# Branches for an expert's further blocks taken once per unit of weights, and their activations transposed in the next pass

## The chip, the core and the metric

The kernel runs on one core of a Trainium2 chip. Its time is the device time of one launch, in microseconds (us); a lower one is better. The engines are TensorE (PE; its weight loads are shown apart, as PEld, and its sequencer as PEldq), VectorE (DVE), ScalarE (ACT), GpSimd (POOL) and SyncE (SP), which here only issues DMAs. Each engine has an instruction stream of its own; they meet at semaphores.

## The reference

One decoder layer on 512 tokens of 1024 channels, in float32. After a token-mixing sub-layer (two attentions, some 500 us here, not touched) comes a mixture of 32 experts of which each token uses four:

```python
top_val, top_idx = lax.top_k(logits, TOP_K)            # 4 of 32, softmax weights
padded = (counts + MOE_BLOCK - 1) // MOE_BLOCK * MOE_BLOCK   # groups by expert, blocks of 128 rows
def expert_block(args):
    xb, e = args                                       # 128 tokens of expert e
    gu = xb @ w_gate_up[e] + b_gate_up[e]              # 1024 -> 2048
    return clamped_swiglu(gu) @ w_down[e] + b_down[e]  # 1024 -> 1024
```

How many tokens an expert gets is known only at run time: 2048 token slots over 32 experts, 64 on the mean, one to four blocks of 128 each.

## The kernel before

**Tiling.** An expert's weights come as 12 halves of 1 MB (512 rows by 512 columns each): eight for gate and up, four for down. Two halves make a unit, one output of 128 tokens by 512 columns. For float32 accuracy each half is split into a high and a low part: ACT copies it to `wh` (L1154, a ring of four), DVE subtracts (L1225, in place of the raw half, a ring of eight), and `multiply` (L1048) issues 12 matrix multiplications for a half and a block: high by high, low by high, high by low, over four chunks of 128 rows. A bias matmul (L1057) opens each unit.

**Passes.** `passes` (L940) runs the experts: number 0 by itself, then a loop of 15 passes with two experts each, then number 31 and a tail. In the pass of expert e, PE runs gate and up of e, transposes the tokens of e+1 (`tokens_transposed`, L996), runs down of e-1 and transposes the activations of e (`act_transposed`, L1027). The token blocks are gathered and scattered by POOL.

**Further blocks.** Nearly all experts have one block (b = 0). Code for b = 1, 2, 3 stands in the program all the same, inside nested run-time branches (`further`, L908: `with self.eng.If(self.more >= 1)`). `x.blocks(work)` puts the further blocks ahead of block 0, `x.first_then_further(work)` behind it. PE calls it for each half (`gate_up_half_used` eight times, `down_half_used` four times) and for both transposes, so PE has 14 such branches an expert, all on line L909; for an expert with one block each of them jumps over its code. The wait for the half's low part (`wl_done`) stands ahead of the branch. The loop's own branch is on L943; a hint at the loop's top names it.

**Order.** Everything is in the order of the code; nothing is scheduled. `half_used` frees a half's place for the next load (SP, L973) and for ACT's next copy.

Of the kernel before, what the change touches and what calls it, by code (L numbers as in the profile page):

```python
# [23 lines left out]
P = 128  # L24
# [8 lines left out]
E = 32  # L33
# [58 lines left out]
def program(nc, ctx, x, c, rel_bias_table, w_ada, b_ada, g_mix_pre, g_mix_post, g_ffn_pre, g_ffn_post, w_in, w_out,  # L92
# [895 lines left out]
    def experts_pe(pe):  # L988
        pe.wait_ge(nk_ready, 1)

        def transposed(b, src, done):
            for k in range(KC):
                ins = nc.tensor.transpose(turned(b)[:, k // 4, (k % 4) * P:(k % 4 + 1) * P], src[:, k * P:(k + 1) * P], ident[:])  # L993
            ins.then_inc(done[min(b, 1)], 1)

        def tokens_transposed(x, e):  # L996
# [5 lines left out]
            def work(b):  # L1002
                if b == 0:
                    pe.wait_ge(xg_in[0], (e + 1) * 16)
                else:
                    if b == 1 and not begins:
                        acts = Expert(pe, e - 1).prefix() + START
                        if not (isinstance(e, int) and e == 1):
                            outputs = Expert(pe, e - 2).prefix() * U_D + START
                        pe.wait_ge(al_done[1], acts)  # L1010
# [10 lines left out]
                transposed(b, xy[b], xt_done)  # L1021
# [37 lines left out]
        def gate_up_half_used(x, has_d, place, v):  # L1059
            t, up, h = v // 4, v // 2 % 2, v % 2  # L1060
            pe.wait_ge(wl_done, place.count(v))

            def work(b):
                dst = summed(b, up)
                if v == 0 and b == 0:
                    pe.wait_ge(xl_done[0], x.count(1, 0, 0))
                if v == 0 and b:
# [6 lines left out]
                if h == 0:  # L1074
                    if b == 0:
                        if t == 0 and has_d:
                            pe.wait_ge(y_half_copied[up], x.e - 1 + START)
                        elif t:
                            pe.wait_ge((u_ready if up else g_ready)[0], x.count(T_GU, 0, 0))
# [10 lines left out]
                elif h:  # L1090
                    ins.then_inc(gu_more, 1)
# [755 lines left out]
```

## Time and profile before

| | us |
|---|---|
| median of 3 runs | 1965.25 |
| lowest, highest | 1964.48, 1971.41 |
| profiled execution: device time | 1966.11 |
| its span in the trace | 1964.3 |
| PE busy in the span | 1700.9 |
| expert loop, from PE's first to its last matmul in it | about 514 to 1900 |

The profile comes from one execution. A row of PE's timeline gives a matmul's start and its modelled length; since matmuls overlap, the distance from one start to the next is what it costs. "issue" as the releaser of an idle time means that the trace shows nothing that the engine waited for. Branches and register instructions are the sequencer's, and are not counted as busy, but their own lengths can be read on their lines.

### The profile page before, as it was taken

The page shows a single profiled execution, that of the slowest core. Times are in us where ns is not written, and L with a number is a line of the kernel's source. Part 1 is how long each engine was busy: PE and PEld are TensorE (multiplying, and loading weights), DVE is VectorE, ACT ScalarE, POOL GpSimd, SP SyncE. Part 2 cuts the span into 40 slices and gives each one's busy share as a digit, 9 for nine tenths or more (in the row PEclk, how much of TensorE's full clock was granted, in tenths as well). Part 3 has the DMA queues.
Part 4 walks back from the last instruction along what each step waited for, and adds up shares of the span by engine and source line. Part 5 has one row for each costly group of instructions (what it writes and reads, how often), then busy time and mean ns, then how long its engine had stood idle before and what let it go on. Part 6 is the DMA issues. An engine that isn't in the chain of part 4 may idle for free.

```text
span 1964.3 us, 24736 instructions
## 1 busy us (share of the span) xinstructions
PE 1700.9 (87%) x7526; PEld 1315.3 (67%) x7527; DVE 1317.5 (67%) x1024; ACT 1029.6 (52%) x922; POOL 229.2 (12%) x232
## 2 busy tenths in 40 slices
PE   6999976685488999999999999999999998989860
PEld 1788854443376877787777877878787787778650
DVE  0444468644478778586877877866687787566645
ACT  2322234511366766465766766745576676455530
POOL 2000000102201001011111101101100111001110
PEclk9999987797699999999999999999999999999885
DMA  7675440012689999687989988977798899667735
GB/s 230 218 246 185 150 120 1 28 65 76 230 300 333 326 327 337 221 300 279 353 309 323 353 315 319 370 255 259 273 373 317 315 362 331 219 237 274 274 135 220
DMA packets 245582, 498.81 MB, mean 254 GB/s; under 512 B 16795, under 2 KB 17927, under 8 KB 244737
## 3 DMA queue, kind: packets, MB, share of 16 engines
q1 hardware_dynamic: 228288, 458.26, 65.5%
q0 software_dynamic: 14448, 34.73, 5.2%
q8 instruction: 217, 3.56, 0.7%
q10 hardware_dynamic: 2610, 2.11, 0.3%
q14 instruction: 19, 0.16, 0.0%
HBM read 490.23 MB, written 27.09 MB: 263 GB/s over the span
## 4 chain that ended last, share of the span: by engine, by line
PE 69%; issue 5%; DVE 3%; DMA 2%; ACT 1%; POOL 1%; POOLq 0%; ACTq 0%; DVEq 0%
PE ps L1051 20%; PE ps L1052 20%; PE ps L1053 19%; PE ps L621 3%; PE ps L993 3%; PE ps L1057 3%; DMA x1e<-x_after_mixing 1%; ACT wh L1154 1%; DVE wl L1225 1%; DMA xy<-h_ffn,icur 1%; DMA expert_rows<-xy,icur 1%; PE ps L641 0%; DVE yo L1388 0%; PE ps L634 0%; ACT h2t L692 0%
## 5 line engine op out<-in xcount | busy, mean ns | idle before, releaser
L1225 DVE TENSOR_TENSOR wl<-rawm,wh 128x2048 fp32r<-128x2048 f32 x384 | 876.2, 2290 | 318.9 <-ACT wh L1154 316.9
L1154 ACT ACTIVATE wh<-rawm 128x2048 fp32r<-128x2048 f32 x384 | 736.2, 1918 | 488.9 <-PE ps L1053 488.8
L1051 PE MATMUL ps<-wh,xh 128*128 128x512 f32 x1120 | 477.8, 427 | 0.0
L1052 PE MATMUL ps<-wl,xh 128*128 128x512 f32 x1120 | 447.4, 399 | 0.0
L1053 PE MATMUL ps<-wh,xl 128*128 128x512 f32 x1120 | 446.3, 399 | 0.0
L1053 PEld LDWEIGHTS ps<-wh,xl 128*128 128x128 f32 x1120 | 216.9, 194 | 48.2
L1052 PEld LDWEIGHTS ps<-wl,xh 128*128 128x128 f32 x1120 | 217.9, 195 | 45.6
L1051 PEld LDWEIGHTS ps<-wh,xh 128*128 128x128 f32 x1120 | 219.3, 196 | 41.6
L1051 PE MATMUL ps<-wh,ah 128*128 128x512 f32 x560 | 235.0, 420 | 0.0
L1052 PE MATMUL ps<-wl,ah 128*128 128x512 f32 x560 | 220.4, 394 | 0.0
L1053 PE MATMUL ps<-wh,al 128*128 128x512 f32 x560 | 220.1, 393 | 0.0
L1331 POOL COPY icur<-stab 128x1 int32 (+1 forms) x35 | 49.6, 1417 | 1026.4 <-ACT xy L1194 1026.3
L1057 PE MATMUL ps<-bparts,sel 96*128 96x512 bf16 x210 | 85.1, 405 | 70.3 <-issue 54.8
L1053 PEld LDWEIGHTS ps<-wh,al 128*128 128x128 f32 x560 | 106.4, 190 | 23.3
L1052 PEld LDWEIGHTS ps<-wl,ah 128*128 128x128 f32 x560 | 106.8, 191 | 21.9
L1051 PEld LDWEIGHTS ps<-wh,ah 128*128 128x128 f32 x560 | 107.5, 192 | 20.3
L1711 DVE TENSOR_TENSOR wlf<-raw,whf 128x2048 fp32r<-128x2048 f32 (+1 forms) x18 | 39.1, 2174 | 100.7 <-ACT whf L1487 100.7
L1057 PEld LDWEIGHTS ps<-bparts,sel 96*128 (+1 forms) x210 | 20.5, 98 | 115.3 <-issue 110.3
L1590 PE MATMUL ps<-whf,hh 128*128 128x512 f32 (+1 forms) x192 | 71.3, 372 | 0.0
L1592 PE MATMUL ps<-whf,hl 128*128 128x512 f32 (+1 forms) x192 | 71.1, 370 | 0.0
L1591 PE MATMUL ps<-wlf,hh 128*128 128x512 f32 (+1 forms) x192 | 71.0, 370 | 0.0
L993 PE MATMUL ps<-ident,xy 128*128 128x128 f32 x280 | 38.4, 282 | 33.2 <-DMA xy<-h_ffn,icur 26.8
(224 smaller groups left out, 1658.2 us busy)
## 6 DMA issues: line engine op xcount, KB each, us to landing
rawm<-in_w_gate_up SPq DMA_DIRECT2D x256, 1024.0 KB, 6.6
rawm<-in_w_down SPq DMA_DIRECT2D x128, 1024.0 KB, 6.3
raw<-in_w_ada SPq DMA_DIRECT2D x24, 1024.0 KB, 5.3
raw<-in_w_in SPq DMA_DIRECT2D x16, 1024.0 KB, 5.2
yt<-expert_rows POOLq DMA_DIRECT2D x4, 2048.0 KB, 9.1
wo<-in_w_out SPq DMA_DIRECT2D x2, 2048.0 KB, 17.0
bias_vectors_repeated<-bias_vectors POOLq DMA_DIRECT2D x1, 2304.0 KB, 15.8
xs<-in_x ACTq DMA_DIRECT2D x1, 2048.0 KB, 24.5
```

Of the source, the lines that this page charges most:

```text
L621: ins = nc.tensor.matmul(ps[:, 2 * b + half, :], src[:, k, t * P:(t + 1) * P], wo[:, 4 * b + k, half * UN:(half + 1) * UN], start=(k == 0) ...
L993: ins = nc.tensor.transpose(turned(b)[:, k // 4, (k % 4) * P:(k % 4 + 1) * P], src[:, k * P:(k + 1) * P], ident[:])
L1051: nc.tensor.matmul(dst, a_h[:, b, kk, :], wh[:, place.split(v), k, :], start=False, stop=False)
L1052: nc.tensor.matmul(dst, a_h[:, b, kk, :], wl[:, place.slot(v), k, :], start=False, stop=False)
L1053: ins = nc.tensor.matmul(dst, a_l[:, b, kk, :], wh[:, place.split(v), k, :], start=False, stop=kk == KC - 1)
L1057: nc.tensor.matmul(dst, sel[:, bass.ds(e, 1)].to_broadcast([96, P]), bias, start=True, stop=False)
L1154: nc.scalar.activation(flat(wh[:, place.split(v), :, :]), flat(rawm[:, place.slot(v), :, :]), ACT.Copy).then_inc(wh_done, 1)
L1225: nc.vector.tensor_tensor(flat(wl[:, place.slot(v), :, :]), flat(rawm[:, place.slot(v), :, :]), flat(wh[:, place.split(v), :, :]), ALU.sub ...
L1331: nc.gpsimd.tensor_copy(icur[:, 1, b:b + 1], stab[:, b, bass.ds(x.e + 1, 1)]).then_inc(scur[m], 1)
L1590: nc.tensor.matmul(dst, a_h, b_h, start=first, stop=False)
L1591: nc.tensor.matmul(dst, a_h, b_l, start=False, stop=False)
L1592: return nc.tensor.matmul(dst, a_l, b_h, start=False, stop=last)
```

## The change

On PE the work of an expert is asked for once per unit and not once per half: `gate_up_used` (four calls) and `down_used` (two) have one branch each for the further blocks, with both halves of the unit inside it, then block 0 with both halves. The wait for a half's low part now stands ahead of that half's own matmuls. The first block's activations are transposed inside the second down unit, between its halves (`first_act_transposed`). Those of the further blocks are transposed in the next pass, ahead of its second unit (`further_act_transposed`, a branch of its own), and a branch ahead of the fourth unit waits that they are split (`further_acts_split`). ACT and DVE split them behind the second half of the next pass. The further blocks' activations all use the same two PSUM banks. PE now has nine branches an expert instead of 14. No matmul, transpose, copy or DMA is added or removed. `multiply` and `biased` are as they were.

```diff
--- before.py
+++ after.py
-        def transposed(b, src, done):
+        def transposed(banks, src, done):
             for k in range(KC):
-                ins = nc.tensor.transpose(turned(b)[:, k // 4, (k % 4) * P:(k % 4 + 1) * P], src[:, k * P:(k + 1) * P], ident[:])
-            ins.then_inc(done[min(b, 1)], 1)
+                ins = nc.tensor.transpose(banks[:, k // 4, (k % 4) * P:(k % 4 + 1) * P], src[:, k * P:(k + 1) * P], ident[:])
+            ins.then_inc(done, 1)
...
-        def act_transposed(x, last):
+        def first_act_transposed(x, last):
 
             pe.wait_ge(xl_done[0], x.e + (1 if last else 2) + START)
-
+            pe.wait_ge(act_ready[0], x.count(T_GU, 1, 0))
+            transposed(turned(0), actv[:, 0, :], at_done[0])
+
+        def further_act_transposed(x):
             def work(b):
-                if b == 1:
-                    tokens = x.before + x.more if last else Expert(pe, x.e + 2).prefix()
-                pe.wait_ge(act_ready[min(b, 1)], x.count(T_GU, 1, b))
-                if b == 1:
-                    pe.wait_ge(xl_done[1], tokens + START)
-                    pe.wait_ge(y_copied[1], x.before * U_D + START)
-                if b == 2:
-                    pe.wait_ge(al_done[0], x.count(1, 0, 0))
-                if b == 3:
-                    pe.wait_ge(al_done[1], x.count(1, 0, b) - 2)
-                transposed(b, actv[:, b, :], at_done)
-                if b == 2:
-                    pe.wait_ge(al_done[1], x.count(1, 0, b))
-                    pe.sem_inc(passed, 1)
-            x.first_then_further(work)
+                pe.wait_ge(act_ready[1], x.count(T_GU, 1, b))
+                pe.wait_ge(al_done[0], x.count(1, 0, 0))
+                pe.wait_ge(al_done[1], x.count(1, 0, b) - 1)
+                transposed(turned(0), actv[:, b, :], at_done[1])
+            x.further(work)
+
+        def further_acts_split(x):
+            with pe.If(x.more >= 1):
+                x.prefix()
+                pe.wait_ge(al_done[1], x.all_more(1, 0))
+                pe.sem_inc(passed, 1)
...
-        def gate_up_half_used(x, has_d, place, v):
-            t, up, h = v // 4, v // 2 % 2, v % 2
-            pe.wait_ge(wl_done, place.count(v))
-
-            def work(b):
+        def gate_up_used(x, has_d, place, v):
+            t, up = v // 4, v // 2 % 2
+            bias = bparts[:, up * D + UN * t:up * D + UN * (t + 1)]
...
-                ins = multiply(dst, place, v, b, h, xh, xl)
-                if b == 0:
-                    ins.then_inc(half_used, 1)
-                elif h:
-                    ins.then_inc(gu_more, 1)
-            x.blocks(work)
+                if b == 1 and t:
...
+                biased(dst, x.e, bias)
+                for h in range(2):
+                    pe.wait_ge(wl_done, place.count(v + h))
+                    ins = multiply(dst, place, v + h, b, h, xh, xl)
+                ins.then_inc(gu_more, 1)
+            x.further(further)
+
+            if v == 0:
+                pe.wait_ge(xl_done[0], x.count(1, 0, 0))
+            if t == 0 and has_d:
+                pe.wait_ge(y_half_copied[up], x.e - 1 + START)
+            elif t:
+                pe.wait_ge((u_ready if up else g_ready)[0], x.count(T_GU, 0, 0))
+            biased(summed(0, up), x.e, bias)
+            for h in range(2):
+                pe.wait_ge(wl_done, place.count(v + h))
+                multiply(summed(0, up), place, v + h, 0, h, xh, xl).then_inc(half_used, 1)
...
-            x.blocks(work)
+            x.further(further)
+
+            if t == 0:
+                pe.wait_ge(al_done[0], x.count(1, 0, 0))
+            pe.wait_ge((u_ready if t else g_ready)[0], (x.e + (1 if after is None else 2)) * T_GU + START)
+            biased(summed(0, t), x.e, bias)
+            for h in range(2):
+                if t and h and after is not None:
+                    first_act_transposed(after, is_last(after.e))
+                pe.wait_ge(wl_done, place.count(v + h))
+                multiply(summed(0, t), place, v + h, 0, h, ah, al).then_inc(half_used, 1)
...
             last = is_last(e)
-            for v in range(N_GU):
-                if v == N_GU - 1:
+            before = None
+            for v in range(0, N_GU, 2):
+                if v == 2 and has_d:
+                    before = Expert(pe, e - 1)
+                    further_act_transposed(before)
+                if v == 6:
+                    if has_d:
+                        further_acts_split(before)
                     nxt = None if last else Expert(pe, e + 1)
-                gate_up_half_used(x, has_d, place, v)
+                gate_up_used(x, has_d, place, v)
             if not last:
                 tokens_transposed(nxt, e + 1)
-            before = Expert(pe, e - 1) if has_d else None
-            for d in range(N_D if has_d else 0):
-                down_half_used(before, x, place, N_GU + d, d)
-            act_transposed(x, last)
+            if has_d:
+                for t in range(U_D):
+                    down_used(before, x, place, N_GU + 2 * t, t)
+            else:
+                first_act_transposed(x, last)
 
         passes(pe, body)
         end = Expert(pe, E - 1)
-        for d in range(N_D):
-            down_half_used(end, None, LAST, d, d)
+        further_act_transposed(end)
+        for t in range(U_D):
+            down_used(end, None, LAST, 2 * t, t)
...
-        def act_high(x):
+        def act_high(x, blocks):
             def work(b):
                 m = min(b, 1)
                 act.wait_ge(at_done[m], x.count(1, 0, b))
-                nc.scalar.activation(flat(ah[:, b, :, :]), flat(turned(b)), ACT.Copy).then_inc(ah_done[m], 1)
-            x.first_then_further(work)
+                nc.scalar.activation(flat(ah[:, b, :, :]), flat(turned(0)), ACT.Copy).then_inc(ah_done[m], 1)
+            blocks(work)
...
                 split_high(place, v + SPL)
+                if v == 1 and has_d:
+                    act_high(before, before.further)
                 if v in (1, 5):
                     gate(x, v // 4, place, v)
                 if v == 7 and not is_last(e):
@@ -1212,10 +1226,11 @@
                     tokens_high(after)
                 if v in (9, 11):
                     outputs(before, v // 2 - 4, place, v, after)
-            act_high(x)
+            act_high(x, at_once)
 
         passes(act, body)
         end = Expert(act, E - 1)
```

DVE's part is the same as ACT's (`act_low` instead of `act_high`).

On PE, at the end of the loop's body, before: the last matmul of the second down unit's block 0, then the eight transposes, the branch, and (behind its code) the loop's branch.

```order
L1053 MATMUL ps<-wh,al 128x512
L1029 REGISTER_ALU
L1034 REGISTER_ALU
L993 MATMUL ps<-ident,actv 128x128 x8
L909 COMPARE_AND_BRANCH
...
L913 UNCONDITIONAL_BRANCH
L943 REGISTER_ALU
L943 COMPARE_AND_BRANCH
L874 TENSOR_LOAD nk
```

The same place after the change: the transposes stand between the two halves of that unit, and twelve matmuls stand ahead of the loop's branch.

```order
L1050 MATMUL ps<-wh,al 128x512
L1027 REGISTER_ALU
L1028 REGISTER_ALU
L993 MATMUL ps<-ident,actv 128x128 x8
L1122 REGISTER_ALU
L1048 MATMUL ps<-wh,ah 128x512
...
L1050 MATMUL ps<-wh,al 128x512
L943 REGISTER_ALU
L943 COMPARE_AND_BRANCH
L874 TENSOR_LOAD nk
```

So the transposes moved ahead of twelve matmuls, and one branch left the end of the body.

On PE, between the tokens' transposes and the first down unit of the second expert, after the change (before it, two register rows more stood ahead of the second branch, L1097 among them, and one half's code behind it):

```order
L1050 MATMUL ps<-wh,xl 128x512
L1004 REGISTER_ALU
L993 MATMUL ps<-ident,xy_111 128x128 x8
L909 COMPARE_AND_BRANCH
...
L913 UNCONDITIONAL_BRANCH
L909 COMPARE_AND_BRANCH
L877 ISA
...
L1054 MATMUL ps<-bparts,sel 128x512
L1110 REGISTER_ALU
L1048 MATMUL ps<-wh,ah 128x512
```

What follows the second branch is now a whole unit's code for three further blocks.

## Rows read from the trace of the kernel before

**Rows 1.** Page, parts 1 and 4: busy time, chain by engine.

```profile
PE 1700.9 (87%) x7526; PEld 1315.3 (67%) x7527; DVE 1317.5 (67%) x1024; ACT 1029.6 (52%) x922; POOL 229.2 (12%) x232
...
PE 69%; issue 5%; DVE 3%; DMA 2%; ACT 1%; POOL 1%; POOLq 0%; ACTq 0%; DVEq 0%
```

**Rows 2.** Groups of PE instructions, 600 to 1890 us: count, busy, mean ns, idle before.

```profile
L1057 PE MATMUL ps<-bparts,sel 96*128 96x512 bf16 x196 | 79.0, 403 | 59.7 <-issue 54.6 <-DVE wl L1225 5.2
```

**Rows 3.** Windows, a loop edge and the pass behind it: engines, clock, DMA.

```profile
core 0: us, PE busy (x) PEld busy (x) DVE busy (x) ACT busy (x) POOL busy (x), PEclk, DMA share, GB/s
1057.20:1061.90 4.70, 0.97 (x9) 0.73 (x7) 4.27 (x3) 3.31 (x3) 1.50 (x1) 0.85 1.04 383
1061.90:1067.10 5.20, 5.17 (x13) 4.07 (x14) 0.80 (x1) 0.00 (x0) 1.28 (x3) 0.50 0.26 96
1067.10:1135.40 68.30, 68.30 (x313) 55.24 (x312) 58.83 (x34) 50.23 (x33) 6.25 (x5) 1.00 0.97 346
```

**Rows 4.** Timeline of PE at the second edge: start, length, instruction, idle before.

```profile
1135.42 1.04 PE L993 MATMUL ps<-ident,actv 128*128 128x128 f32 x8
1140.93 0.60 PE L1057 MATMUL ps<-bparts,sel 96*128 96x512 bf16 x1 [4.47 <-issue]
1140.97 0.99 PE L1051 MATMUL ps<-wh,xh 128*128 128x512 f32 x1
1141.76 0.63 PE L1052 MATMUL ps<-wl,xh 128*128 128x512 f32 x1
...
1145.60 0.51 PE L1052 MATMUL ps<-wl,xh 128*128 128x512 f32 x1
1145.95 0.40 PE L1053 MATMUL ps<-wh,xl 128*128 128x512 f32 x1
```

**Rows 5.** One line, L909: branches, count, shortest/median/longest ns, first and last start.

```profile
L909 PEldq COMPARE_BRANCH  x448: 73/227/5450, 514.4 to 1896.5; - x150
```

**Rows 6.** L909 in eight short windows, one branch each (the fourth: two), same columns.

```profile
L909 PEldq COMPARE_BRANCH  x1: 201/201/201, 521.6 to 521.6; - x1
...
L909 PEldq COMPARE_BRANCH  x1: 347/347/347, 523.8 to 523.8; - x1
...
L909 PEldq COMPARE_BRANCH  x1: 355/355/355, 1065.1 to 1065.1; - x1
...
L909 PEldq COMPARE_BRANCH  x2: 222/330/438, 1097.3 to 1098.3; - x2
...
L909 PEldq COMPARE_BRANCH  x1: 2173/2173/2173, 1102.1 to 1102.1; - x1
...
L909 PEldq COMPARE_BRANCH  x1: 360/360/360, 1117.3 to 1117.3; - x1
...
L909 PEldq COMPARE_BRANCH  x1: 1052/1052/1052, 1121.9 to 1121.9; - x1
...
L909 PEldq COMPARE_BRANCH  x1: 4590/4590/4590, 1136.0 to 1136.0; - x1
```

**Rows 7.** L943, the loop's own branch: all fifteen, then the one at 1133.6.

```profile
L943 PEldq COMPARE_BRANCH  x15: 89/769/3537, 626.7 to 1842.8; - x15
...
L943 PEldq COMPARE_BRANCH  x1: 1316/1316/1316, 1133.6 to 1133.6; - x1
```

**Rows 8.** DMA queues, 1057 to 1136 us: packets, MB, share of 16 engines.

```profile
q8 instruction: 13, 0.21, 1.0%
```

**Rows 9.** Timeline of PE while the branch at 1102.1 waits.

```profile
1102.20 0.39 PE L1052 MATMUL ps<-wl,xh 128*128 128x512 f32 x1
...
1105.83 0.39 PE L1053 MATMUL ps<-wh,xl 128*128 128x512 f32 x1
```

**Rows 10.** Groups of other engines in the loop, and the count of blocks (page, part 5).

```profile
L1154 ACT ACTIVATE wh<-rawm 128x2048 fp32r<-128x2048 f32 x359 | 688.6, 1918 | 468.6 <-PE ps L1053 468.6
...
L1331 POOL COPY icur<-stab 128x1 int32 (+1 forms) x35 | 49.6, 1417 | 1026.4 <-ACT xy L1194 1026.3
```

More of the change, by code:

```diff
@@ L1087, in work @@
-                ins = multiply(dst, place, v, b, h, xh, xl)
-                if b == 0:
-                    ins.then_inc(half_used, 1)
-                elif h:
-                    ins.then_inc(gu_more, 1)
-            x.blocks(work)
-        def down_half_used(x, after, place, v, d):
-            t, h = d // 2, d % 2
-            pe.wait_ge(wl_done, place.count(v))
-            def work(b):
+                if b == 1 and t:
+                    pe.wait_ge((u_ready if up else g_ready)[1], x.count(T_GU, 0, b))
+                elif b > 1 and up:
+                    pe.wait_ge(g_ready[1], x.count(T_GU, t, b))
+                elif b > 1 and t:
+                    pe.wait_ge(u_ready[1], x.count(T_GU, 0, b))
@@ L1100, in work, with down_used, further @@
+            biased(summed(0, up), x.e, bias)
+            for h in range(2):
+                pe.wait_ge(wl_done, place.count(v + h))
+                multiply(summed(0, up), place, v + h, 0, h, xh, xl).then_inc(half_used, 1)
+        def down_used(x, after, place, v, t):
+            bias = bparts[:, 2 * D + UN * t:2 * D + UN * (t + 1)]
+            def further(b):
                 dst = summed(b, t)
-                if d == 0 and b == 0:
-                    pe.wait_ge(al_done[0], x.count(1, 0, 0))
@@ L1103, in work @@
-                if d == 0 and b:
+                if t == 0:
                     gate_ups = x.before + x.more if after is None else x.before + x.more + after.more
@@ L1196, in outputs, with at_once @@
             x.blocks(work)
+        def at_once(work):
+            work(0)
         tokens_high(Expert(act, 0))
@@ L1214, in body @@
                     outputs(before, v // 2 - 4, place, v, after)
-            act_high(x)
+            act_high(x, at_once)
         passes(act, body)
         end = Expert(act, E - 1)
+        act_high(end, end.further)
         outputs(end, 0, LAST, 1, None)
@@ L1234, in tokens_low, with act_low @@
             x.first_then_further(work)
-        def act_low(x):
+        def act_low(x, blocks):
             def work(b):
@@ L1239, in work @@
                 dve.wait_ge(ah_done[m], x.count(1, 0, b))
-                nc.vector.tensor_tensor(flat(al[:, b, :, :]), flat(turned(b)), flat(ah[:, b, :, :]),
+                nc.vector.tensor_tensor(flat(al[:, b, :, :]), flat(turned(0)), flat(ah[:, b, :, :]),
                                         ALU.subtract).then_inc(al_done[m], 1)
-            x.first_then_further(work)
+            blocks(work)
         def up(x, t, place, v):
@@ L1267, in experts_dve, with at_once @@
         dve.wait_ge(nk_ready, 1)
+        def at_once(work):
+            work(0)
         tokens_low(Expert(dve, 0))
@@ L1280, in body @@
                 split_low(place, v + SPL)
+                if v == 1 and has_d:
+                    act_low(before, before.further)
             if not has_d:
                 tokens_low(Expert(dve, e + 1))
-            act_low(x)
+            act_low(x, at_once)
         passes(dve, body)
+        end = Expert(dve, E - 1)
+        act_low(end, end.further)
     def experts_pool(pool):
```

41 lines of the change are left out of this document (11 added, 30 removed).

## The prediction, made before the changed kernel ran

> **What bounds the kernel now.** I read the page first: PE is busy 87% of the span, and the chain that ended last is 69% PE and 5% "issue" [rows 1]. So PE's gaps in the expert loop are the place to look. The groups of PE's instructions in the loop put nearly all of them in one group, the bias matmul that opens a unit: 59.7 us of idle time, 54.6 of it "issue", and only 5.2 behind DVE's low parts [rows 2]. The timeline shows where: the eight activation transposes at the end of a pass start at 1135.42, and the next matmul at 1140.93, after 4.47 us idle [rows 4]. The windows show the price behind it: at the edge before that one PE idles in 1057.2 to 1061.9 and then runs at a granted clock of 0.50 (1.2 GHz) until 1067.1; after that PE is busy 68.30 of 68.30 us at 1.00 (2.4 GHz) [rows 3]. At the half clock a matmul costs 0.43 us from start to start, else 0.23 ([rows 4], 1141.76 to 1145.60 is nine of them).
>
> What PE waits for is its sequencer, in branches. L909 has 448 of them (32 experts by 14), median 227 ns, longest 5450 [rows 5]; the one at 1136.0 took 4590, and its end, 1140.6, is the end of PE's gap [rows 4, 6]. These long ones are waits for code. A pass moves 13 instruction packets of together 0.21 MB, 16 KB each [rows 8]. I counted PE's program in its order (a matmul as two instructions, jumps to the next instruction left out): the loop body of two experts is numbers 3060 to 6165, 3106 instructions, so a packet holds about 256 of them (0.21 MB / 3106 is 68 bytes), and all code is fetched once per pass, the skipped code too.
>
> Three kinds of branches in [rows 6] give the rule. (1) Inside a code block: 201 and 222 ns. (2) Into the next block, already there: 347 to 438. (3) Into a block that isn't there yet: the wait ends some 5.5 us after the block before it was entered. Entered at 1098.7, next one there at 1104.3 (branch at 1102.1): 5.6. Entered 1117.7, next there 1123.0: 5.3. The loop's branch ends at 1134.9 [rows 7] and the first one of the pass at 1140.6: 5.7. So one block is fetched ahead, and two block edges must be 5.5 us apart in the sequencer's time. Where are the edges? The branch at 523.8 starts at instruction 2140, 92 past a multiple of 256, and is of kind 2; that at 521.6 lands 66 past one and is of kind 1; that at 1065.1 lands 73 past one and is of kind 2. So an edge lies more than 92 past, and the sequencer reads some 20 to 30 instructions ahead: the edge is at 93 to about 103 past each multiple.
>
> A wait of the sequencer costs PE nothing while PE's queue lasts. At 1102.1 the branch waits 2.17 us and PE shows no gap: 17 matmuls (1102.20 to 1105.83) were still in the queue [rows 9]. That is 17 x 0.227 = 3.9 us of cover.
>
> **The change, part by part (per pass of two experts, 15 passes).**
>
> *Fewer branches.* Nine instead of 14 an expert. One inside a block costs 0.22 us of sequencer time, which the queue hides: 0 us. At the body's end one goes that stood in the open: -0.25.
>
> *Transposes ahead of twelve matmuls.* At the edge the queue held 9 matmuls and 8 transposes, 9 x 0.227 + 8 x 0.11 = 2.9 us; now 17 matmuls, 3.9 us. The gap shrinks by 1.0. PE's own work is the same. ACT copies them behind its last split and output as before, and ACT idles 468.6 us for PE [rows 10]: 0 us, and at most one 1.9 us copy if it came late.
>
> *The loop's top.* A jump is now 161 to 187 instructions long (before: 78 to 114). The first one goes from 2965 to 3152, 80 past a multiple: inside the 20 to 30 instructions ahead of the edge, so it is again of kind 3, as before. 0 us.
>
> *The loop's end.* The body is now 2960 to 5984. 5984 is 96 past a multiple of 256, at or beside an edge. If the edge is at 96 or lower, the loop's branch is the first instruction of a block, which the sequencer enters about 24 instructions, 12 matmuls or 2.7 us, before it. The loop's top is fetched from when that block is entered (before: entered 5.5 us ahead, and the branch took 0.77 us in the median, 1.3 in this pass [rows 7]). Now it waits 5.5 - 2.7 = 2.8 us and takes 3.1. Added: 3.1 - 0.8 = 2.3. No row shows this place. Bounds: -0.5, if the top is there and the branch is of kind 2 (some 0.35 instead of 0.8), and +5.2, if the fetch begins at the branch itself (5.5 + 0.4 less 0.8). I take the value between them that the reading ahead gives.
>
> *Tokens to down unit, second expert.* The branch behind the tokens' transposes jumps over an edge (5455 to 5525), and the next, 0.6 us later, jumps 174 instructions to 5699, at the next edge. The first of the two edges is entered about four transposes earlier, when the queue is full: 1.3 us before. So the sequencer waits about 4.2 us there with 3.9 - 0.6 - 0.4 = 2.9 us in the queue: a gap of 1.3 us, bounds 0 and 2.4. Before, the edges there were 4 us apart and the wait of 1.05 [rows 6] was hidden. At the first expert's tokens the edges come 3 us apart, the wait of about 1.5 to 2.5 stays hidden.
>
> *The low part's wait* moved behind the branch: PE waited 5.2 us in all for DVE [rows 2]; 0, at best -3. *Further blocks*: 35 blocks for 32 experts [rows 10], so three experts; their transposes and splits move, none is added: 0, within 3 us either way. *Tail*: the jump behind the loop took 5450 ns [rows 5]; after the change it stays in its block and the wait comes 20 matmuls later, partly hidden: -4.
>
> *Sum.* -0.25 - 1.0 + 2.3 + 1.3 = +2.35 a pass, 15 passes: +35; tail -4: +31. From the profiled execution, 1966.1: 1997. The median of the runs is 0.9 lower: 1996. The clock term stays (the gap at the edge grows to some 5 us, and it already pays the half clock).
>
> **The rivals.**
> A. *The edge lies just past the loop's branch* (97 to 103). Then the top of the loop is there early; the edge term is -0.5 instead of +2.3, so a pass changes by -0.25 - 1.0 - 0.5 + 1.3 = -0.4: -6, with the tail 1956; with a gap of 2 us at the tokens, 1966. For it: half of the interval of edges. Against: the sequencer reads ahead over that edge too, and may have to fetch it first.
> B. *The same, and the clock holds.* The edge's gap falls from about 4 to 2.5 us. If that no longer drops the clock, 12 matmuls cost 0.23 instead of 0.43: another -2.4 a pass, -36: 1925. Against: DMA share is already 0.97 with PE busy [rows 3], so a faster pass is soon bound by the loads.
> C. *Both waits in a row* (slower, further). At the loop's end the sequencer needs the block past the edge and the loop's top, one after the other, each 5.5 us, before the first block of the pass: a pass gets +5 instead of +2.35, 1966 + 75 - 4 = 2037. It decides if the edge is within the 24 instructions behind the branch.
> D. *Only distance counts*, not how soon one code edge follows another. Then neither the loop's end nor the place behind the tokens gets a new wait, and the cover alone is left: -1.25 a pass, -19: 1943 with the tail. Against: the waits of 2.17 and 1.05 us are at jumps of 87 and 100 instructions, to the very next block [rows 6]. This is what the Trainium skill says in "Runtime: NRT & Kernel Launch", section "Instruction fetch mechanics": code comes in 16 KiB blocks, prefetched in sequence, and a taken branch stalls for a fetch if its target is outside a window of two blocks. By that rule no jump of the new kernel (187 at most) leaves the window. The trace agrees on the block (16 KB a packet), and not on the window as the whole condition.
>
> **How the numbers follow.** Forecast 0.47, its own range 1985 to 2020 (fetch of 5 or 6 us instead of 5.5, and a gap at the tokens of 0 to 2.4). A 0.17, B 0.12, C 0.10, D 0.06, and 0.08 for something unnamed, half on each side. Eight in ten: 1940 to 2030, which leaves out B and half of C. A change of 0.5% (9.8 us) is what this measurement can tell. Slower: 0.47 + 0.10 + 0.04 = 0.61. Faster: B, D, 0.04 and a fifth of A: 0.25 (0.12 + 0.06 + 0.04 + 0.03). Within 0.5%: 0.14.
>
> **What would show it.** In the profile after, L943 should have a median of about 3 us instead of 0.77. PE's idle time ahead of the bias matmul should be near 5 us at the edge, with a new gap of 1 to 2 us ahead of the first down unit of every second expert, the L909 branch there near 4 us. "issue" ahead of the bias matmul should grow from 54.6 to about 90. An L943 median under 0.5 speaks for A or B, clock 1.00 throughout a pass for B. I am wrong if code isn't fetched as I read it: if L909 at the top of a pass is short, or if there are no long branches at those two places.

## The result, and the profile after

The changed kernel takes 2043.72 us (median of 4 runs, 2039.56 to 2050.01), the kernel before 1968.26 beside it (1964.48 to 1971.41): a ratio of 1.0387, 95% interval 1.0349 to 1.0425. It is slower, as forecast, but by 75 us instead of 31, and outside the range. The profiled execution has a span of 2044.1 us; before it was 1964.3.

The page of the changed kernel, busy time and chain by engine, and the group of bias matmuls (L1054 is the L1057 of before) in the loop:

```profile
PE 1725.0 (84%) x7526; PEld 1326.5 (65%) x7527; DVE 1316.5 (64%) x1024; ACT 1028.7 (50%) x922; POOL 223.9 (11%) x232
...
PE 66%; issue 8%; DMA 3%; DVE 2%; ACT 1%; POOL 1%; POOLq 0%; ACTq 0%; DVEq 0%
```

```profile
L1054 PE MATMUL ps<-bparts,sel 96*128 96x512 bf16 x198 | 81.0, 409 | 117.8 <-issue 112.3 <-DVE al L1255 5.5
```

Against [rows 1, 2], "issue" ahead of this group went from 54.6 to 112.3 us. L1048 and L1049 have 7.1 us of it that their lines did not have before, and L993 has 1.8 where it had 6.4: +60.2 in all. PE is also busy 24.1 us longer for the same 7526 matmuls. Together that is 84.3, of which other waits give 4.5 back: the span grew by 79.8.

The timeline of PE in one pass has three such gaps (start, length, instruction, idle before); before, there was one in a pass [rows 4]:

```profile
1145.50 0.39 PE L1050 MATMUL ps<-wh,xl 128*128 128x512 f32 x1
1147.31 0.39 PE L1054 MATMUL ps<-bparts,sel 96*128 96x512 bf16 x1 [1.42 <-issue]
...
1164.40 1.03 PE L993 MATMUL ps<-ident,xy 128*128 128x128 f32 x8
1167.31 0.39 PE L1054 MATMUL ps<-bparts,sel 96*128 96x512 bf16 x1 [1.87 <-issue]
...
1180.99 0.39 PE L1050 MATMUL ps<-wh,al 128*128 128x512 f32 x1
1185.48 0.60 PE L1054 MATMUL ps<-bparts,sel 96*128 96x512 bf16 x1 [4.10 <-issue]
```

The first stands ahead of the second expert's first gate unit, the second behind the tokens' transposes (ahead of the second expert's first down unit), the third at the loop's edge. Sorted by these places over all fifteen passes, the timeline gives 19.9 us (5.3 of them inside that unit, in two passes with a further block), 42.2 us (34.7 of them at the second expert) and 55.5 us. Before, it was 0, 2.4 and 52.1. One more wait of before belongs to the edge, although the profile puts it down to DVE (4.4 of the 5.2 us in [rows 2]): the branch ahead of it took 3.8 us and ended 0.35 us before this matmul started. With it the edge had 56.5 us.

```profile
983.44 0.61 PE L1057 MATMUL ps<-bparts,sel 96*128 96x512 bf16 x1 [4.37 <-DVE wl L1225]
```

PE's windows show what a gap costs behind it (columns as in [rows 3]; the last row stands behind the tokens' gap of the next pass):

```profile
1150.00:1164.70 14.70, 14.70 (x67) 11.76 (x67) 11.31 (x8) 10.19 (x7) 1.26 (x2) 1.00 0.98 347
1164.70:1167.30 2.60, 0.74 (x7) 0.50 (x6) 2.56 (x3) 2.60 (x2) 0.00 (x0) 1.00 1.04 369
1167.30:1171.00 3.70, 3.69 (x11) 2.96 (x12) 3.49 (x3) 0.13 (x1) 0.00 (x0) 0.63 0.60 229
...
1185.48:1190.00 4.52, 4.52 (x14) 3.65 (x15) 1.31 (x2) 0.00 (x0) 1.22 (x2) 0.64 0.25 90
...
1250.20:1254.00 3.80, 3.80 (x17) 3.17 (x18) 3.56 (x3) 0.86 (x2) 0.00 (x0) 1.00 0.70 256
```

Behind the tokens' gap of 1.87 us the granted clock is 0.63 in the mean of 3.7 us, that is 1.2 GHz for the greater part of them; behind the one of 1.75 us a pass later it stays at 1.00 (2.4 GHz). This fall stands behind the second expert's tokens in six of the fifteen passes. From the first expert on, the clock is at 1.2 GHz for 145 us before and for 178 us after. At half the clock the added 33 us cost 17, which is the greater part of PE's 24 us of longer busy time.

The sequencer's branches at those places (L909 and L943 in short windows: count, shortest/median/longest ns, first and last start), then all of either line (twelve of L943's fifteen took over 3 us):

```profile
L909 PEldq COMPARE_BRANCH  x2: 355/2431/4507, 1142.3 to 1142.7; - x2
...
L909 PEldq COMPARE_BRANCH  x2: 364/2468/4573, 1162.2 to 1162.6; - x2
...
L943 PEldq COMPARE_BRANCH  x1: 3824/3824/3824, 1178.0 to 1178.0; - x1
...
L909 PEldq COMPARE_BRANCH  x1: 2402/2402/2402, 1182.7 to 1182.7; - x1
...
L909 PEldq COMPARE_BRANCH  x256: 72/232/6144, 517.1 to 1972.1; - x128
...
L943 PEldq COMPARE_BRANCH  x15: 97/3710/3955, 632.5 to 1923.0; - x15
```

L943's median is 3710 ns, where [rows 7] had 769. The queues in two stretches, before the branch at 1142.7 asked for code and while it waits, say what it waits for:

```profile
q1 hardware_dynamic: 991, 1.99, 87.7%
...
q1 hardware_dynamic: 186, 0.35, 77.5%
q8 instruction: 1, 0.02, 5.2%
```

The first is 1138.5 to 1144.6, without an instruction packet; the second 1144.6 to 1145.9, with one. The packet leaves at 1144.8, 2.0 us after the branch began, lands at 1145.9, and the branch ends at 1147.25. PE's queue covers 3.2 of these 4.5 us (its last matmul starts at 1145.50).

This holds for all long branches. TensorE has 947 branches of 0.9 us or more in the experts of the twenty traces on record (50 before, 59 after), and each of them ends 1.1 to 1.7 us after an instruction packet landed; the packets are some 6 us apart, so chance would not do this. What differs is when the packet leaves: in 16 of the 50, and in 40 of the 59, over 0.5 us after the branch began.

### The profile page after: what moved, and what is told of

It is laid out like the page before. It is cut to its first block, busy times and chain, and to the rows that moved or that the text cites. A ratio compares the mean times of both kernels' runs of the same rounds, so it can differ in the third digit from the quotient of the medians.

```text
span 2044.1 us, 24472 instructions
## 1 busy us (share of the span) xinstructions
PE 1725.0 (84%) x7526; PEld 1326.5 (65%) x7527; DVE 1316.5 (64%) x1024; ACT 1028.7 (50%) x922; POOL 223.9 (11%) x232
## 4 chain that ended last, share of the span: by engine, by line
PE 66%; issue 8%; DMA 3%; DVE 2%; ACT 1%; POOL 1%; POOLq 0%; ACTq 0%; DVEq 0%
PE ps L1048 19%; PE ps L1049 19%; PE ps L1050 19%; PE ps L993 3%; PE ps L621 3%; PE ps L1054 3%; DMA xy<-h_ffn,icur 1%; DMA x1e<-x_after_mixing 1%; DMA expert_rows<-xy,icur 1%; PE ps L641 0%; DVE yo L1410 0%; ACT wh L1163 0%; POOL icur L1353 0%; PE ps L634 0%; DVE wl L1240 0%
## 5 line engine op out<-in xcount | busy, mean ns | idle before, releaser
L1048 PE MATMUL ps<-wh,xh 128*128 128x512 f32 x1120 | 479.0, 428 | 7.6 <-issue 5.3
L1049 PE MATMUL ps<-wl,xh 128*128 128x512 f32 x1120 | 449.0, 401 | 1.8 <-issue 1.8
L1048 PEld LDWEIGHTS ps<-wh,xh 128*128 128x128 f32 x1120 | 220.6, 197 | 52.5 <-issue 6.8
L1049 PEld LDWEIGHTS ps<-wl,xh 128*128 128x128 f32 x1120 | 219.9, 196 | 44.4
L1048 PE MATMUL ps<-wh,ah 128*128 128x512 f32 x560 | 241.1, 431 | 0.0
L1049 PE MATMUL ps<-wl,ah 128*128 128x512 f32 x560 | 224.8, 401 | 0.0
L1050 PE MATMUL ps<-wh,al 128*128 128x512 f32 x560 | 224.4, 401 | 0.0
L1054 PE MATMUL ps<-bparts,sel 96*128 96x512 bf16 x210 | 86.1, 410 | 120.2 <-issue 112.3
L1054 PEld LDWEIGHTS ps<-bparts,sel 96*128 (+1 forms) x210 | 20.5, 98 | 174.4 <-issue 165.7
L1049 PEld LDWEIGHTS ps<-wl,ah 128*128 128x128 f32 x560 | 109.4, 195 | 21.3
L1048 PEld LDWEIGHTS ps<-wh,ah 128*128 128x128 f32 x560 | 109.8, 196 | 20.4
L1509 ACT ACTIVATE whf<-raw 128x2048 fp32r<-128x2048 f32 (+1 forms) x18 | 32.7, 1817 | 64.5 <-PE ps L1614 64.5
```

Source lines behind the costliest of these rows:

```text
L1048: nc.tensor.matmul(dst, a_h[:, b, kk, :], wh[:, place.split(v), k, :], start=False, stop=False)
L1049: nc.tensor.matmul(dst, a_h[:, b, kk, :], wl[:, place.slot(v), k, :], start=False, stop=False)
L1050: ins = nc.tensor.matmul(dst, a_l[:, b, kk, :], wh[:, place.split(v), k, :], start=False, stop=kk == KC - 1)
L1054: nc.tensor.matmul(dst, sel[:, bass.ds(e, 1)].to_broadcast([96, P]), bias, start=True, stop=False)
```

## The experiments

Eighteen kernels were run, each beside the kernel before. "Loop" is the time from the first to the last start of L943, fourteen passes; "packets" those of q8 in the run. "Further" means moved by so many instructions.

| kernel | us | ratio (95%) | loop | L943, median ns | packets |
|---|---|---|---|---|---|
| before (1964 to 1969 in the six series) | 1965 | 1 | 1216 | 769 | 217 |
| changed | 2043.7 | 1.0349 to 1.0425 | 1290 | 3710 | 216 |
| changed, all 32 further | 1977.1 | 1.0037 to 1.0094 | 1227 | 3694 | 216 |
| changed, all 64 further | 1935.2 | 0.9763 to 0.9905 | 1186 | 433 | 216 |
| changed, all 128 further | 1935.4 | 0.9767 to 0.9909 | 1184 | 428 | 216 |
| changed, all 192 further | 1927.2 | 0.9712 to 0.9860 | 1169 | 462 | 203 |
| changed, all 256 further | 2060.3 | 1.0463 to 1.0541 | 1288 | 3811 | 217 |
| before, all 64 further | 1981.2 | 1.0056 to 1.0123 | 1227 | 4768 | 217 |
| before, all 128 further | 1974.0 | 1.0016 to 1.0063 | 1227 | 4113 | 217 |
| before, all 192 further | 1965.2 | 0.9968 to 1.0022 | 1199 | 742 | 217 |
| changed, loop's branch 32 further | 2022.2 | 1.0205 to 1.0330 | 1271 | 3366 | 216 |
| from the tokens' branch on | 2024.3 | 1.0264 to 1.0352 | 1259 | 3579 | 216 |
| from the second expert on | 2001.1 | 1.0140 to 1.0213 | 1256 | 3732 | 216 |
| changed, transposes last | 2010.2 | 1.0139 to 1.0293 | 1256 | 968 | 216 |
| the same, all 192 further | 1924.1 | 0.9760 to 0.9829 | 1168 | 441 | 203 |
| before, transposes moved | 1972.2 | 1.0027 to 1.0062 | 1213 | 909 | 217 |
| changed, two blocks' code | 1887.0 | 0.9560 to 0.9636 | 1139 | 221 | 22 |
| before, two blocks' code | 1904.5 | 0.9657 to 0.9736 | 1148 | 226 | 22 |
| changed, three blocks' code | 1900.0 | 0.9620 to 0.9704 | 1155 | 365 | 168 |
| two blocks' code, one far jump | 2000.4 | 1.0135 to 1.0223 | 1250 | 3687 | 150 |

### Where the code lies

The same program is moved as a whole, by 32 to 256 semaphore increments that TensorE executes once, ahead of its experts:

```diff
         pe.wait_ge(nk_ready, 1)
+        for _ in range(64):
+            pe.sem_inc(passed, 1)
```

Expected for 64, 128 and 192 on the changed kernel:

> The changed kernel with 64 semaphore increments on PE ahead of the experts (PE waits there for the first tokens), so that all its later code stands 64 instructions further on; nothing else differs. Theory 1 (the time is lost at edges of 256-instruction code blocks that fall badly: at the loop's branch, ahead of the second expert's first gate unit, and behind its tokens' transposes): the loop's branch is no longer beside an edge, a pass falls from 84 to about 77 us, the kernel to about 1940 (1925 to 1965). Theory 2 (the new order of waits and work itself costs it, wherever the code stands): 2044, within 10.

> The same with 128 instructions. Theory 1: about 1940 again, the long branches at other places than in the changed kernel, or gone. Theory 2: 2044, within 10.

> The same with 192 instructions. Theory 1: about 1940 again, 1900 to 1960. Theory 2: 2044, within 10. Were the times of the three shifts spread by more than 1%, the place of the code would be a larger effect than most edits.

The same on the kernel before:

> The kernel before, with 64 semaphore increments put on TensorE ahead of its experts' code, so that this code lies 64 instructions further on and is the same otherwise. Theory 1 (what counts is where the far branches lie against the code blocks): the place matters for the kernel before as well, so that its three shifts of 64, 128 and 192 spread by over 20 us among themselves, and this one falls between 1940 and 2000. Theory 2 (only the changed code is sensitive, the kernel before isn't): 1960 to 1970 for each of the three.

> The same with 128 increments. Theory 1: here the loop's branch and several of the branches over the further blocks come to lie late in their blocks; 1960 to 2030, the slowest of the three shifts. Theory 2: 1960 to 1970.

> The same with 192 increments. Theory 1: 1915 to 1955, the fastest of the three; if it comes to within 10 us of the changed kernel shifted by 192 (1927), the change is worth nothing once both lie well, and if it stays at 1950 or above, the change is worth over 20 us. Theory 2: 1960 to 1970.

The changed kernel falls by 108 to 117 us and is then faster than before, as theory 1 has it. The kernel before gets 1981, 1974 and 1965 us, a spread of 16 where over 20 was expected. So place matters for it too, by up to 0.9%, but far less. That 128 would be its slowest shift, and that 192 would bring it down to 1955 or less, was wrong. The changed kernel 192 further on, two of TensorE's groups that have "issue", and two windows that cover most of a pass:

```profile
L1051 PE MATMUL ps<-wl,xh 128*128 128x512 f32 x1120 | 439.7, 393 | 12.7 <-issue 12.7
...
L1056 PE MATMUL ps<-bparts,sel 96*128 96x512 bf16 x210 | 83.5, 397 | 14.2 <-issue 5.9 <-DVE al L1257 5.5 <-DVE xl L1249 2.4
```

```profile
1125.00:1150.00 25.00, 25.00 (x114) 19.96 (x113) 21.73 (x12) 18.07 (x14) 5.53 (x4) 1.00 0.99 362
1150.00:1190.00 40.00, 40.00 (x188) 32.35 (x186) 35.88 (x22) 29.67 (x21) 5.82 (x4) 1.00 1.00 361
```

PE is busy without a gap at the full clock, and the DMA engines are too: such a pass takes 72 us, not 78 (before) or 84 (after). Here each pass fetches 12 packets, and 13 at the shifts of 64 and 128. The 12.7 us at L1051 are waits for code as well, in seven passes, but without a branch: a unit's code is run straight on, and PE stops in its middle. This one ends 1.4 us after a packet landed (at 1061.3), as the branches do:

```profile
1059.60 0.39 PE L1050 MATMUL ps<-wh,xh 128*128 128x512 f32 x1
1062.73 0.50 PE L1051 MATMUL ps<-wl,xh 128*128 128x512 f32 x1 [2.75 <-issue]
```

A shift of a whole block and one of an eighth:

> The changed kernel, shifted by 256 instructions, a whole block. Theory 1 (only the place within the blocks counts): every wait of the changed kernel comes back at its place, 2030 to 2055. Rival (the place from the program's start or the amount of work ahead of the experts counts, and any shift breaks an unlucky pattern): 1925 to 1980, as the other shifts.

> The changed kernel with the 32 increments ahead of all the experts' code: everything in the loop lies 32 further on, its top as well. Theory 1: the top's branch has its target behind the block's edge too; 1930 to 1965, as the shifts by 64 to 192. Rival: 2040 to 2050, as nothing is jumped over that was not before; a shift of so little (half of 64) would then have to show nothing.

At 256 everything comes back in the loop: it takes 1288 us (1290 unshifted), and the same branches wait. The whole takes 2060, past the 2055 that was expected. Its 17 us over the changed kernel lie ahead of the loop's first branch, which starts at 646.9 instead of 632.5, behind the 256 increments. At 32, over half of the loss is gone already, though not down to the 1965 that was expected at most. So what counts is where the code stands against blocks of 256.

### One place after another

Increments in the code for a fourth block, which no expert has here, move what stands behind them and are never executed; the first of three places, the others stand likewise in the code of the transposes:

```diff
                 ins.then_inc(d_more, 1)
+                if b == 3 and t == 1 and after is not None and place.r == 4:
+                    for _ in range(32):
+                        pe.sem_inc(passed, 1)
```

> The changed kernel with 32 semaphore increments in the code for a fourth block in the second expert's last down unit, which no expert has on these inputs: nothing more is executed, and of the whole loop only its own branch (L943) lies 32 instructions further on, with the code behind it. Theory 1 (a branch waits by where it and its target lie against the code blocks): L943, which took 3.5 us on average, takes under 1.5 and the gap at the loop's edge shrinks by 1 to 2 us a pass; 2010 to 2030. Rival (the distances that the code jumps over, or its volume, decide): the branch over the padded code jumps over 32 more, and the time is 2044 or above.

> The same 32 increments further ahead instead, in the fourth block's code of the second expert's token transposes: the branch ahead of its first down unit and everything behind it in the loop lie 32 further on. Theory 1: besides L943 the wait ahead of the second expert's first down unit (4.8 us, gaps of 1.3 to 4.9) goes, 1.5 to 3 us a pass more; 1975 to 2005. Rival: 2044 or above.

> The same 32 increments still further ahead, in the fourth block's code of the activations' transposes in the second expert's gate and up units, so that the branch that took 3.9 us there and everything behind it lie 32 further on. Theory 1: its gap of 1.3 to 2.2 us goes as well, unless one of the branches that are now moved comes to lie badly; 1950 to 1980. Rival: 2044 or above.

All three are faster than the changed kernel, so the rival (2044 or above) fell. But only the first lies in its range: 2022, then 2024 (up to 2005 expected), 2001 (up to 1980), and 1977 with the whole moved (up to 1965). The second pad brought nothing over the first, and the loop's branch still takes over 3 us in the median, where under 1.5 was expected. And the branch behind the tokens' transposes, at the very same place (from 5557 to 5731, by the prediction's count) in the second and the third kernel, took this long in one pass of each (each window holds a short one too):

```profile
L909 PEldq COMPARE_BRANCH  x2: 353/2433/4513, 1223.5 to 1223.9; - x2
```

```profile
L909 PEldq COMPARE_BRANCH  x2: 234/800/1365, 1223.3 to 1223.6; - x2
```

Over ten passes it is 4.7 us in the one and 1.2 in the other. The place of a branch alone does not decide, then: what the code ahead of it did, and when blocks were fetched for it, does too. In the third kernel another branch, between the pad and this one and short in the second kernel, had waited 4.2 us some 14 us earlier. And the branch ahead of the gate unit, which the third pad was to free, still took 4.4 us in that pass, with its target now behind the edge.

### The moved transposes

Undone in the changed kernel, at the same code length:

```diff
-                if t and h and after is not None:
-                    first_act_transposed(after, is_last(after.e))
...
-            else:
-                first_act_transposed(x, last)
+            first_act_transposed(x, last)
```

> The changed kernel with the first block's transposes back at the end of the body; PE's code keeps its length and every branch its place. Theory 1: only the cover at the loop's edge differs (9 matmuls and 8 transposes in the queue for 17 matmuls), 1.0 us a pass: 2059. Theory 2, if it was the transposes inside the unit that cost: back towards 1990 or below.

> The kernel before, in which only the transposes of the first block's activations move from the end of the expert's body to between the halves of the last down unit; the branches stay one for each half unit, and all code keeps its length. Theory 1 (placement, with the moved transposes worth what the changed kernel's twin lost by undoing it, 2010 against 2044, or nothing): 1965 to 2000, by how the fewer instructions between the branches change when the blocks are asked for. Rival (the transposes, where they stand now, give TensorE more queued work ahead of the branches and so help): 1935 to 1955, that is 1 to 2 us a pass.

> The changed kernel shifted by 192 (1927 us), with the first block's transposes put back at the body's end. Theory 1 (the moved transposes cost only through waits that a bad place gives, and otherwise put queued work behind the weights' arrival): without those waits undoing them costs 5 to 15 us, 1932 to 1945. Rival (they cost by themselves, as the 33 us at the other place suggest): 1890 to 1920.

The moved transposes cost 33 us at the bad place, 6 in the kernel before, and nothing where the code lies well (1927 and 1924, intervals that overlap). So they have no price of their own that these runs show. Theory 1 expected that undoing them costs 15 us at the bad place and 5 to 15 at the good one, and was wrong in both: it gained 33 and 3. The rivals (1990 or below, and 1890 to 1920) expected more gain than there was. In the kernel with the transposes last, L943 waits 0.98 us in place of 3.8, the top's L909 4.6 in place of 2.4, and the edge's gap is nearly the same (rows of its edge):

```profile
L943 PEldq COMPARE_BRANCH  x1: 977/977/977, 1155.8 to 1155.8; - x1
...
L909 PEldq COMPARE_BRANCH  x1: 4640/4640/4640, 1157.8 to 1157.8; - x1
```

```profile
1157.96 1.04 PE L993 MATMUL ps<-ident,actv 128*128 128x128 f32 x8
1162.78 0.39 PE L1054 MATMUL ps<-bparts,sel 96*128 96x512 bf16 x1 [3.78 <-issue]
```

What it saves is mostly the gap ahead of the second expert's gate unit, whose branch now takes 1.7 us: a wait half a pass away from the transposes. Why it is short there is not shown.

### How much code

Both kernels without the code for a third and a fourth block on all engines (a part of the computation that these inputs don't use; a kernel for any input needs it):

```diff
-                for b in range(2, NB):
+                for b in range(2, 2):
```

> The changed kernel without the code for a third and a fourth block on all engines, which no expert has on these inputs; the loop's code on TensorE is 1572 instructions instead of 3024. Theory 1 (the waits come from fetching code that is jumped over): about 6 blocks are fetched in a pass instead of 13, most waits go, and the time is 1890 to 1930. Rival (TensorE is held by something else in those places, and a fetch in a pass more or less is no matter): 1927 to 2044, as the shifts.

> The kernel before without the code for a third and a fourth block, likewise. Theory 1: 1910 to 1945, with fewer waits too; against the changed kernel cut in the same way it tells what the merged branches and the moved transposes are worth alone: 5 to 20 us for the changed one by the 0.25 us of branches a pass and the queued work. Rival: 1955 to 1975, as before.

Six packets a pass were expected, and there are none: they fall from 216 (13 a pass) to 22 in the whole run. A loop of 1572 instructions, or of 1629 in the kernel before so cut, is not fetched again at all. Both times are a little under their ranges. Of the changed kernel so cut, the bias matmuls and a whole pass:

```profile
L1054 PE MATMUL ps<-bparts,sel 96*128 96x512 bf16 x210 | 83.2, 396 | 9.1 <-DVE al L1255 5.5 <-DVE xl L1247 2.4 <-issue 1.2
```

```profile
1000.00:1072.00 72.00, 72.00 (x334) 58.00 (x333) 63.89 (x37) 53.34 (x38) 11.10 (x9) 1.00 0.99 360
```

With no code to wait for in the loop, the change gains 17.5 us. Nine of them are in the loop, and there in passes with further blocks; a plain pass takes 72.0 us in the one and 71.8 in the other. The last two runs:

> The changed kernel without the code for a fourth block alone (no expert has a third or a fourth): the loop's code on TensorE is 2311 instructions, between 1572 (22 fetches in the run, 1887 us) and 3024 (216 fetches, 1927 to 2060 us). Theory 1 (a loop of over some size is fetched anew in every pass, in all its blocks): about 10 fetches a pass, 150 or more in the run, and waits by where the branches lie; 1895 to 1960. Rival (it still stays in the chip): 22 to 40 fetches and 1885 to 1895.

> The changed kernel without the code for a third and a fourth block, with 1400 semaphore increments at the end of the loop that one branch always jumps over: the loop spans 2973 instructions on TensorE, nearly as in the full kernel, but only 1573 of them are run through or stand between the other branches. Theory 1 (only the blocks that are run through count): 22 to 40 fetches in the run, and 1885 to 1895. Rival (the extent of the loop counts): the loop's blocks are fetched anew in every pass, 100 fetches or more, with waits at the long jump and at the loop's branch; 1900 to 1960.

```diff
+            if place.r == 4:
+                with pe.If(nxt.more >= 3):
+                    for _ in range(1400):
+                        pe.sem_inc(passed, 1)
```

With a third block's code (2311 instructions) ten blocks are fetched in a pass, and it costs 13 us: fetching is cheap where the queue covers the waits, as it does in nearly all passes of this run. With the far jump, theory 1 fell: the loop is fetched anew, and the time is beyond the 1960 that its rival gave at most. Its rows at one edge, the long jump (L1149), the loop's branch behind it, and PE:

```profile
L1149 PEldq COMPARE_BRANCH  x1: 4242/4242/4242, 1227.2 to 1227.2; - x1
...
L943 PEldq COMPARE_BRANCH  x1: 4159/4159/4159, 1231.6 to 1231.6; - x1
```

```profile
1230.38 0.39 PE L1050 MATMUL ps<-wh,al 128*128 128x512 f32 x1
1237.27 0.60 PE L1054 MATMUL ps<-bparts,sel 96*128 96x512 bf16 x1 [6.51 <-issue]
```

All other branches of its pass are short. Two waits in a row are the whole loss: 113 us over fifteen edges, 7.6 each, of which 6.5 are PE's gap in this pass; PE is also busy 22 us longer in the run (1704.0 after 1681.6). Whether the loop's extent (2973) or the number of blocks it asks for (nine a pass) makes the chip fetch it anew, this run does not tell.

One rival to "the block was asked for late" is that its packet stood behind the weights' packets in busy DMA engines. One of the long jumps was made with these engines idle. It still took 3.89 us, and its packet left 1.5 us after it began; the other fourteen took 3.7 to 5.3 us. So most of such a wait is there without other traffic. What traffic adds to the longest ones is not shown.

```profile
L1149 PEldq COMPARE_BRANCH  x1: 3893/3893/3893, 1428.9 to 1428.9; - x1
```

```profile
1426.00:1428.90 2.90, 2.90 (x16) 2.35 (x15) 0.00 (x0) 0.03 (x1) 0.00 (x0) 1.00 0.00 0
1428.90:1430.40 1.50, 1.50 (x12) 1.37 (x11) 0.00 (x0) 1.50 (x1) 0.00 (x0) 1.00 0.02 8
```

The Trainium skill, "Runtime: NRT & Kernel Launch", section "Instruction fetch mechanics", gives TensorE a store of 2048 instructions, filled in blocks of 256 in order. The runs agree: loops of 1572 and 1629 stay, one of 2311 does not. So the chip holds more code than the two blocks of rival D's rule: a loop of 1629 instructions is seven blocks.

## Why the prediction was wrong

The direction came true, but partly by luck. The term that made the forecast slower, +2.3 at the loop's end, is about zero, and the loss stands at two places that had 1.3 together in the sum, and in the clock, which had nothing.

- *What bounds the kernel, and the unit of fetching*: right. Blocks of 256 (the shift by 256 gives the loop's time back to 0.2%), thirteen packets in a pass (12 to 14), waits in branches, covered by the queue. Waits in code without a branch come beside them.
- *"The wait ends some 5.5 us after the block before it was entered"*: this is the step that failed, and with it the sizes. From the packet's start to the branch's end it is nearly always the same, 2.3 to 3.0 us in both kernels. What the rule had wrong is when the packet starts. In the three rows that it was read from, this is 2.9 to 3.3 us after the block before was entered. After the change, at the loop's edge, the packet for the top left at 1179.4, 1.4 us after the branch began; the next one 0.7 us after that block was entered (1181.8), and the wait ended 3.35 us after the entry, not 5.5. Where the block had not been asked for, the wait in this pass was 4.5 to 4.6 us from the branch (2.0 to 2.2 to the packet's start, 1.0 for it, 1.4 until the branch ends), and up to 6.1 in others. What sets the packet's start stays open.
- *The loop's end, +2.3*: the place was right and L943 took 3.8 us (3.1 forecast, 3.7 in the median). But the top's branch, forecast unchanged at 4.6, took 2.4. From L943's start to the end of the top's wait it is 7.2 us now and was 7.0 [rows 6, 7]. The gap is 4.10 after 4.47, since the queue covered 3.4 us in place of 2.9: this term is about zero, and the -1.0 for the cover was 0.5 in this pass. Over all passes the edges' gaps are 55.5 us after 56.5, so the two together are -0.1 a pass.
- *Tokens to down unit, +1.3*: right in place and kind (4.57 us of wait for 4.2 forecast, cover 2.9 as forecast, gap 1.87), mis-sized over the run: 42.2 us after 2.4, +2.7 a pass, of which 0.4 stand at the first expert's tokens, where the wait was to stay hidden. In other passes the branch took up to 6.1.
- *The second expert's first gate unit*: missed altogether. Its branch (4785 to 4946 by the same count) ends just short of the edge that I put near 4960; I had applied that very test at the loop's top and not here. 19.9 us of idle time, +1.3 a pass. In the run that moves its target behind the edge it still waits, so the edge alone isn't the reason.
- *The clock stays*: wrong. In six passes a second stretch at 1.2 GHz stands behind the tokens' gap, and PE is busy 24 us longer, 1.6 a pass; some 17 us of it are the clock.
- *Fewer branches and more cover, -1.25 a pass or -19*: 17.5 us with no code waits in the way, but not where I put it (9 in the loop, the rest outside). *The tail, -4*: the gap behind the loop's end fell only from 3.5 to 1.8 us, and from L943's last start to the end it is 121 us in both. *The low part's wait, at best -3*: of the 5.2 us for DVE's weights, 4.4 were a wait for code at the loop's edge, so only 0.8 could go.
- *Sum*: +2.35 a pass forecast. Measured over fifteen passes: -0.1 at the edge, 2.7 at the tokens, 1.3 at the gate unit, 1.6 of longer busy time, -0.2 for the rest: 5.3. (The upper bound of the loop's end, 5.5 + 0.4 less 0.8, is +5.1 and not +5.2, which bears on nothing.)
- *Rival C* (2037) was nearest in time and wrong here: both waits stand in a row at the loop's edge, but did before as well. The far jump shows its mechanism alone, at 7.6 us. *Rival A* came true elsewhere: with the loop's code 64 to 192 further on the loop's branch is short, at 1927 to 1935 against its 1956 (and B's 1925, clock 1.00 through the pass; by B's own terms, 1956 less 36, it should have been 1920). *Rival D*, that only the distance of a jump counts, is wrong: the new jumps of 161 and 174 instructions wait 4.5 us each in the pass shown, though neither goes further than the next block, and in the shifted kernels, where all distances are the same, the median of L943 goes from 3710 to 433 ns.

Not settled: when exactly the chip asks for the next block. The same branch at the same place waits 4.7 or 1.2 us by what came before, so edges alone, as I counted them, can't forecast a time. The gap between the best and the worst place in the blocks of one program, 1927 and 2044, is larger than the 17.5 us that the change is worth without waits for code. The measured verdict on it is one on its place: with its code 192 further on, the full computation takes 1927.2 us, faster than both kernels (ratio to before 0.9786).

## What to carry to other kernels

When "issue" stands ahead of the first matmul behind a branch, look at the branches' times and the instruction packets before judging a reordering: run the kernel shifted by 64, 128 and 192 instructions, and compare best with best. Keep a hot loop's code, rarely used blocks included, small enough that it isn't fetched again (here 1629 instructions of TensorE's stayed and 2311 did not), since that was worth 40 us against the best place and 157 against the one that the change came with. A skip is paid for when its target's block was not yet asked for. Where that happens could not be read from the block edges alone, so measure it. A queue that holds 3 us of matmuls does not cover a wait of 4.5 us.

## What the runs showed that I had not expected

- A branch to code that wasn't asked for takes 3.8 to 4.6 us in the passes shown and up to 6.1 in the run; two in a row leave PE idle for 6.5 us. All long branches end 1.1 to 1.7 us after a packet landed.
- Code that is run straight on can wait too, without a branch: 12.7 us at the best place.
- Code that never runs can cost as much as code that does: 1400 increments behind one branch, 113 us.
- A loop that stays in the chip is fetched once: 22 packets in a run instead of 216.
- A 72 us pass has DMA at 0.99 to 1.00 and PE at 1.00 at once: both kernels end there when the code waits are gone.
